# Output projection of a hybrid decoder layer: the recurrence half computed ahead of and among the first attention steps

## The reference, cut to what matters

```
h = rmsnorm(x, norm_g) * (1 + scale) + shift        # shift, scale, gate from c
z = h @ w_in                                        # xr, gr, q, k, v, ga, qi, ki, wi
y_r = rg_lru(conv(xr)) * silu(gr)                   # 512 channels, a recurrence along the sequence
y_a = dsa_attention(q, k, v, qi, ki, wi) * silu(ga) # 8 heads of 64, top-256 keys by an index score
y = concat([y_r, y_a], axis=-1) @ w_out             # 1024 x 1024
x = x + gate * y
return rmsnorm(x, final_g)
```

## Time and profile before

| what | value |
|---|---|
| time, median of 3 runs | 620.57 us (620.45 to 621.84) |
| profiled execution | 619.93 us, span 618.1 us |
| mean granted TensorE clock | 0.926 |
| busy: PE / DVE / ACT / POOL | 535.4 / 439.5 / 377.4 / 233.5 us |
| first transposes of stage 2 | 365.76 us |
| scores of step 16 (first of tile 4) | 406.32 us |
| scores of step 24 (first of tile 7) | 437.19 us |
| last matmul of the output projection ends | about 610.8 us |

### The profile page before, as it was taken

One profiled execution on the slowest core, in us unless ns is written; L12 is line 12 of the kernel. 1 busy time (PEld: TensorE's weight loads), 2 busy tenths in 40 slices (PEclk: granted clock), 3 DMA queues, 4 the chain that ended last, 5 costly groups with the idle time before them and its releaser, 6 DMA issues.

```text
span 618.1 us, 8029 instructions
## 1 busy us (share of the span) xinstructions
PE 535.4 (87%) x2676; PEld 444.8 (72%) x2676; DVE 439.5 (71%) x992; ACT 377.4 (61%) x679; POOL 233.5 (38%) x195
## 2 busy tenths in 40 slices
PE   1459989998999999999999526489999999999994
PEld 1346868777787777778888415478889999888873
DVE  5987386885999889898697886854475666664522
ACT  6513236453499999987898555554466666656531
POOL 5150862352344274677642003740402030313322
PEclk9859999998999999999999855569999999999999
DMA  8967342430112111135550420110011000101011
GB/s 335 418 206 266 105 118 53 102 85 18 36 34 69 34 36 34 35 103 137 140 133 0 177 96 0 68 36 2 8 61 43 28 36 34 41 30 69 0 69 68
DMA packets 16457, 51.96 MB, mean 84 GB/s; under 512 B 4000, under 2 KB 5024, under 8 KB 15392
## 3 DMA queue, kind: packets, MB, share of 16 engines
q1 hardware_dynamic: 16416, 51.45, 26.3%
HBM read 37.81 MB, written 4.19 MB: 68 GB/s over the span
## 4 chain that ended last, share of the span: by engine, by line
PE 68%; DVE 11%; DMA 7%; POOL 5%; ACT 4%; issue 3%; SPq 2%; DVEq 0%; POOLq 0%; ACTq 0%
PE pair L1373 30%; PE pair L1470 13%; PE pair L1492 6%; PE pair L1505 5%; DMA ada<-in_ada_w 4%; PE pair L1448 3%; PE pair L1449 2%; DMA qs<-half_lo 2%; PE pair L1422 2%; DVE rank L1156 2%; PE pair L1514 2%; PE pair L1413 2%; PE pair L1414 2%; DVE tie L1158 1%; POOL half_lo L726 1%
## 5 line engine op out<-in xcount | busy, mean ns | idle before, releaser
L1373 PE MATMUL pair<-h_hi,w_hi 128*128 128x512 f32 (+1 forms) x352 | 114.4, 407 | 1.6 <-DVE h_lo L1064 1.5
L1373 PE MATMUL pair<-h_lo,w_hi 128*128 128x512 f32 (+1 forms) x352 | 109.8, 393 | 0.0
L1373 PE MATMUL pair<-h_hi,w_lo 128*128 128x512 f32 (+1 forms) x352 | 109.0, 391 | 0.0
L1298 DVE TENSOR_TENSOR pt_lo<-pair,pt_hi 128x512 fp32r<-128x512 f32 (+3 forms) x96 | 50.5, 554 | 71.1 <-ACT pt_hi L963 70.5
L858 ACT ACTIVATE bias_sb<-score_sb,tinies 128x1024 bf16<-128x1024 f32 (+2 forms) x93 | 95.7, 1032 | 3.2 <-DVE tinies L1109 3.1
L696 POOL TENSOR_SCALAR w_hi<-w_raw 128x1024 fp32r<-128x1024 f32 (+1 forms) x22 | 29.4, 1339 | 136.3 <-PE pair L1373 120.5
L1373 PEld LDWEIGHTS pair<-h_hi,w_hi 128*128 128x128 f32 (+1 forms) x352 | 65.0, 188 | 19.0 <-issue 6.2
L1373 PEld LDWEIGHTS pair<-h_lo,w_hi 128*128 128x128 f32 (+1 forms) x352 | 66.0, 188 | 15.5 <-issue 0.8
L1373 PEld LDWEIGHTS pair<-h_hi,w_lo 128*128 128x128 f32 (+1 forms) x352 | 65.6, 186 | 15.4 <-issue 0.7
L1095 DVE TENSOR_SCALAR_CACHE_REDUCE bias_sb<-score_sb,tinies 128x640 bf16<-128x640 f32 (+2 forms) x93 | 72.6, 802 | 0.9
L781 POOL TENSOR_TENSOR x_res<-q_free,x_res 128x512 f32<-128x512 f32 x14 | 18.1, 1296 | 121.0 <-DVE q_free L1269 121.0
(11 more groups left out here) (195 smaller groups left out, 1254.2 us busy)
## 6 DMA issues: line engine op xcount, KB each, us to landing
w_raw<-in_w_tiles SPq DMA_DIRECT2D x21, 512.0 KB, 3.5
ada<-in_ada_w SPq DMA_DIRECT2D x8, 1024.0 KB, 18.4
x_sb<-in_x SPq DMA_DIRECT2D x8, 512.0 KB, 7.1
ada_g<-in_ada_w SPq DMA_DIRECT2D x8, 512.0 KB, 4.5
qs<-half_hi SPq DMA_DIRECT2D x16, 256.0 KB, 3.6
qs<-half_lo SPq DMA_DIRECT2D x16, 256.0 KB, 4.4
wo_raw<-in_w_out SPq DMA_DIRECT2D x8, 512.0 KB, 6.4
x_res<-in_x SPq DMA_DIRECT2D x8, 512.0 KB, 3.3
```

Source lines behind the costliest of these rows:

```text
L1298: nc.vector.tensor_tensor(pt_lo[:, 4 * b:4 * b + nc4, hh, :], psum[use % 2][:, 0:nc4 * P].rearrange("p (c q) -> p c q", q=P), f32(pt_hi[:, ...
L1373: ins = nc.tensor.matmul(psum[banks[half]][0:width, :], w[b][:, k, 0:width], hh[:, k, half * HALF:(half + 1) * HALF], start=(k == 0 and p ...
```

## The change

The recurrence half (m < 4) leaves the pieces. For each tile ti and column half it becomes a part of 12 matmuls, e = 2 ti + half, 16 parts. Parts 0 to 3 stand on TensorE ahead of step 0, part g+4 in step g for g = 0 to 11, behind the scores. ScalarE copies each part to SBUF, SP stores it in the rows of the output, where the final result will later overwrite it. In stage 2 the stored rows are loaded back, GpSimd multiplies them with the gate and adds them to x_res (base_of), and what follows is as before. The pieces now hold m = 4 to 7: four a tile, one in every second step from 8 ti + 14 on, for the last tile one a step in 70 to 73. w_out's hi for the slabs 0 to 3 is made by GpSimd, for 4 to 7 by ScalarE in steps 2 to 5. yr_hi of the first two tiles is made at the end of stage 1. The diff, cut to its core:

```diff
-WO_START = 5
-OUT_START = 20
-PIECES = {g: [2 * (g - OUT_START), 2 * (g - OUT_START) + 1] for g in range(OUT_START, 2 * OUT_START - LAG_OUT)}
-PIECES.update({g: [g - LAG_OUT] for g in range(2 * OUT_START - LAG_OUT, LAST_STEP)})
+FIRST_PARTS = 4
+PARTS = 2 * NT
+WO_POOL = CT
+WO_START = 2
+PIECES = {8 * ti + LAG_OUT + 1 + (2 * p if ti < NT - 1 else p): [4 * ti + p] for ti in range(NT) for p in range(4)}
...
+        add("ACT", ("yrh", b), 0.7, 1, ("kstep", NJ - 2 + b, KC - 1), ("yr", CT - 1))
...
+        def part_bank(e):
+            return 2 if e < FIRST_PARTS and e % 2 else 3
...
@@ sync @@
+            for e in range(PARTS):
+                ti, half = divmod(e, 2)
+                i = ATT[ti]
+                sp.wait_ge(part_ev, e + 1)
+                sp.dma_start(out[i * P:(i + 1) * P, half * HALF:(half + 1) * HALF], part[half][:, :]).then_inc(part_out[half], 16)
+            def part_load(ti):
+                i = ATT[ti]
+                for half in range(2):
+                    sp.wait_ge(part_out[half], 16 * (ti + 1))
+                sp.dma_start(part_in[ti % 2][:, :], out[i * P:(i + 1) * P, :]).then_inc(part_back[ti % 2], 16)
...
+            sp.wait_ge(part_ps, PARTS)
             for ti in range(2):
                 sp.dma_start(x_res[ti][:, :], x[ATT[ti] * P:(ATT[ti] + 1) * P, :]).then_inc(xres_in[ti], 16)
+                part_load(ti)
...
                     sp.dma_start(x_res[ti % 2][:, :], x[nxt * P:(nxt + 1) * P, :]).then_inc(xres_in[ti % 2], 16)
+                    sp.wait_ge(base_ok, ti + 1)
+                    part_load(ti + 2)
@@ gpsimd @@
+            def split_wo(m):
+                if m < WO_POOL:
+                    pool.wait_ge(wo_in[m], 16)
+                    nc.gpsimd.tensor_scalar(wo_hi[:, m, :], wo_raw[:, m, :], 1.0, 0.0, ALU.mult, ALU.add).then_inc(wo_hi_ok, 1)
+                pool.wait_ge(wo_hi_ok, m + 1)
+                nc.gpsimd.tensor_tensor(wo_lo[:, m, :], wo_raw[:, m, :], f32(wo_hi[:, m, :]), ALU.subtract).then_inc(wo_ok, 1)
             split_yr(0)
-            split_yr(1)
+            for m in range(WO_POOL):
+                split_wo(m)
+            for ti in range(1, 4):
+                split_yr(ti)
+            for ti in range(4, NT):
+                split_wo(ti)
+                split_yr(ti)
+            def base_of(ti):
+                b = ti % 2
+                pool.wait_ge(part_back[b], 16 * (ti // 2 + 1))
+                nc.gpsimd.tensor_tensor(part_in[b][:, :], part_in[b][:, :], gate_bc[:, :], ALU.mult).then_inc(part_mul, 1)
+                pool.wait_ge(xres_in[b], 16 * (ti // 2 + 1))
+                pool.wait_ge(part_mul, ti + 1)
+                nc.gpsimd.tensor_tensor(x_res[b][:, :], x_res[b][:, :], part_in[b][:, :], ALU.add).then_inc(base_ok, 1)
+            base_of(0)
...
                     nc.gpsimd.tensor_tensor(xs, xs, fg_bc, ALU.mult).then_inc(fin_ok, 1)
+                    base_of(ti + 1)
@@ scalar @@
+            def part_evac(e):
+                ti, half = divmod(e, 2)
+                act.wait_ge(part_ps, e + 1)
+                if ti:
+                    act.wait_ge(part_out[half], 16 * ti)
+                nc.scalar.activation(part[half][:, :], bank(part_bank(e)), ACT.Copy).then_inc(part_ev, 1)
+                if half and ti + 2 < NT:
+                    yr_half(ti + 2)
+            for e in range(FIRST_PARTS - 1):
+                part_evac(e)
             for g in range(LAST_STEP + 1):
+                if 0 <= g + FIRST_PARTS - 1 < PARTS:
+                    part_evac(g + FIRST_PARTS - 1)
...
@@ vector @@
                         if half == 0:
-                            dve.wait_ge(xres_in[ti % 2], 16 * (ti // 2 + 1))
+                            dve.wait_ge(base_ok, NT)
@@ tensor @@
+            def part_of(e):
+                ti, half = divmod(e, 2)
+                i = ATT[ti]
+                if e < 2:
+                    pe.wait_ge(evac_done, len(EVAC) - 1)
+                elif e <= FIRST_PARTS:
+                    pe.wait_ge(part_ev, e - 1)
+                else:
+                    pe.wait_ge(part_ev, e)
+                if half == 0:
+                    pe.wait_ge(yr_ok, ti + 1)
+                for m in range(CT):
+                    if e == 0:
+                        pe.wait_ge(wo_ok, m + 1)
+                    y2 = (yr_hi[ti % 2][:, m, :], yr_lo[:, m, i * P:(i + 1) * P])
+                    for p, (y, w) in enumerate(((y2[0], wo_hi), (y2[0], wo_lo), (y2[1], wo_hi))):
+                        ins = nc.tensor.matmul(bank(part_bank(e)), y, w[:, m, half * HALF:(half + 1) * HALF],
+                                               start=(m == 0 and p == 0), stop=(m == CT - 1 and p == 2))
+                ins.then_inc(part_ps, 1)
+            for e in range(FIRST_PARTS):
+                part_of(e)
...
                     ins.then_inc(att_ps, 1)
+                if g + FIRST_PARTS < PARTS:
+                    part_of(g + FIRST_PARTS)
```

More of the change, by code:

```diff
@@ L227, in stages @@
     add("DVE", ("prep",), 3.5, 2, ("nonneg", len(PICK) - 1))
+    for b in range(2):
+        add("ACT", ("yrh", b), 0.7, 1, ("kstep", NJ - 2 + b, KC - 1), ("yr", CT - 1))
     add("ACT", ("sign",), 3.0, 2, (("prep",), -2.5))
@@ L402, in layer_kernel @@
         x_res = [sb("x_res0", R_R, [P, D]), sb("x_res1", R_S, [P, D])]
-        yr_hi = [sb(f"yr_hi{b}", R_S + 4096 + 2048 * b, [P, CT, P], F32R) for b in range(2)]
+        yr_hi = [sb(f"yr_hi{b}", R_W + 18432 + 2048 * b, [P, CT, P], F32R) for b in range(2)]
+        part = [sb(f"part{b}", R_W + 12288 + 2048 * b, [P, HALF]) for b in range(2)]
         pv_sb = [sb(f"pv{b}", R_R + 4096 + 1024 * b, [P, 2, P]) for b in range(2)]
@@ L419, in layer_kernel @@
         yr_lo = sb("yr_lo", R_YR, [P, CT, S], F32R)
+        part_in = [sb(f"part_in{b}", R_YR + 4096 * b, [P, D]) for b in range(2)]
         ga = sb("ga", R_GA, [P, 4, S])
@@ L548, in layer_kernel @@
         yr_ok = sem("yr_ok")
+        part_ps = sem("part_ps")
+        part_ev = sem("part_ev")
+        part_out = [sem(f"part_out{b}") for b in range(2)]
+        part_back = [sem(f"part_back{b}") for b in range(2)]
+        part_mul = sem("part_mul")
+        base_ok = sem("base_ok")
         att_ps = sem("att_ps")
@@ L663, in _ @@
                     sp.dma_start(x_res[ti % 2][:, :], x[nxt * P:(nxt + 1) * P, :]).then_inc(xres_in[ti % 2], 16)
+                    sp.wait_ge(base_ok, ti + 1)
+                    part_load(ti + 2)
             sp.wait_ge(out_dma, 16 * (NT + 1))
+            for half in range(2):
+                sp.wait_ge(part_out[half], 16 * NT)
         @block.gpsimd
@@ L776, in _ @@
                 if ti < NT - 1:
[L777 removed]
+                    pool.wait_ge(base_ok, ti + 1)
                     for half in range(2):
@@ L958, in _ @@
                         act.wait_ge(pv_ps, pair)
+                    if g - LAG_T == 16:
+                        for b in range(2):
+                            act.wait_ge(part_out[b], 16 * NT)
                     for b in range((keys_of(i) + HALF - 1) // HALF):
@@ L973, in _ @@
                 for o in PIECES.get(g - 1, ()):
-                    if o % 8 == 7 and o // 8 < NT - 1:
-                        ti = o // 8
+                    if o % 4 == 3 and o // 4 < NT - 1:
+                        ti = o // 4
                         act.wait_ge(rstd1_ok, ti + 1)
@@ L979, in _ @@
                 for o in PIECES.get(g, ()):
-                    if o % 4 != 3:
+                    if o % 2 == 0:
                         continue
-                    ti, half = divmod(o // 4, 2)
+                    ti, half = divmod(o // 2, 2)
                     if ti < NT - 1:
@@ L1296, in _ @@
                         nc4 = min(4, i + 1 - 4 * b)
+                        if g - LAG_T == 16 and b == 0:
+                            dve.wait_ge(part_ps, PARTS)
                         dve.wait_ge(t_hi, use_t(use) + 1)
@@ L1450, in _ @@
                     ins.then_inc(att_ps, 1)
+                if g + FIRST_PARTS < PARTS:
+                    part_of(g + FIRST_PARTS)
                 for o in PIECES.get(g, ()):
-                    ti, piece = divmod(o, 8)
-                    i = ATT[ti]
-                    half = piece // 4
-                    if piece % 4 == 0:
-                        if 2 * ti + half:
+                    ti, piece = divmod(o, 4)
+                    half = piece // 2
+                    if piece % 2 == 0:
+                        if o == 0:
+                            pe.wait_ge(part_ev, PARTS)
+                            pe.wait_ge(wo_ok, KC)
+                        else:
                             pe.wait_ge(y_ok, 2 * ti + half)
-                    if ti == 0 and piece < 4:
-                        pe.wait_ge(wo_ok, 2 * piece + 2)
                     if piece == 0:
-                        pe.wait_ge(yr_ok, ti + 1)
-                    if piece == 2:
                         pe.wait_ge(ya_ok, ti + 1)
-                    for m in (2 * (piece % 4), 2 * (piece % 4) + 1):
```

(12 more changed lines are left out.)

35 lines of the change are left out of this document (14 added, 21 removed).

## The result

The changed kernel takes 649.01 us (median of 4 runs, 647.45 to 650.24) where the kernel before takes 620.51 us beside it (619.54 to 621.84): ratio 1.0456, 95% interval 1.0427 to 1.0486, so 28.5 us slower. The forecast was 644.6 us, with a range of 626 to 668. The profiled execution took 649.02 us, with a span of 647.2 us.

What follows compares the result with a forecast made beforehand. The prediction took TensorE to bound the kernel, except in a half-clock hole in attention steps 0 to 15. 620.57 us + 41 (later step 16) - 17 (given back) = 644.6 us, range 626 to 668.

Steps and rivals of the forecast that it cites:

- Step 1: From attention step 16 on: 43.8 us of matmuls leave, odd steps wait for o_sb, 17 us gained (8 to 46).
- Rival (b): Full stretch: odd steps close up because o_sb comes earlier, all 46 us arrive, 616 us; chance 0.07.
- The stand: Tile 7's odd steps: without the piece, TensorE waits 0.87 us for o_sb before the values product.
- Step 2: Start, four parts ahead of step 0: fourth slab ready at 368, transposes of step 1 at 386.4 instead of 365.8.
- the contention price: Start: a w_out slab costs GpSimd 4.6 us beside VectorE's masks, taken three times, against 3.4 alone.
- Step 3: Early attention steps: one part per step without overlap, so step 16 starts 41 us later (33 to 52).
- the ring: Early steps: part, transposes, pt_hi, exponent, evacuation in series, 4.8 us a round; 53.0 us from part 5 to part 15.
- rival (c): Early steps fall to the 1.2 GHz level: 27 us more, 671 us; chance 0.13.
- the way out: From the end of part 15 (439.4) to the start of step 16 (447.4): 8.0 us at full clock.
- Step 4: Loading back, late tiles and end: GpSimd's base_of delays the last add, so 5.5 us fewer matmuls give only 0.5.
- (a): Early steps: the hole hides the parts, only the start's 21 us is lost, 625 us; chance 0.07.
- (d): Whole kernel: parts aren't earlier, or the order differs from what was read: 620 within 2; chance 0.02.

Runs made afterwards that it cites:

- e2: Changed kernel with the recurrence half of the output projection left out altogether, including its stores, loads back and w_out splits: 596.85 us.
- e4: Changed kernel with GpSimd making base_of of the next tile between a tile's two residual adds instead of behind fin: 643.65 us.
- e1: Changed kernel with ScalarE evacuating part g+4 in step g, ahead of pt_hi, instead of in step g+1 behind the exponent: 633.95 us.
- e5: Changed kernel with the four wo_hi copies moved from the end of steps 2 to 5 to directly behind the evacuation: 640.67 us.
- e7: Changed kernel with the first four parts made into four banks at once, row block by row block, and the second tile's recurrence output split first: 641.96 us.
- e10: Changed kernel with four more matmuls, results unused, in each of steps 0 to 14, ahead of the part: 646.05 us.

## Why the prediction held, step by step

**Step 1** (17 us given back) held in mechanism and nearly in size: 14.5 us measured. Tile 4 gained 4.4 (4.4 forecast), tile 7 6.0 (5.9), tiles 6 and 5 2.6 (3.4), tile 3 1.0 (1.0). The term that was most off is the last, tile 2 with the end: 0.5 against 1.9. Rival (b), all 46 us, fell in e2: 24 us even with nothing added. The stand that the forecast read from the rows of tile 7 (0.87 us) came as 0.78: 481.50 less the 480.72 at which the scores' last matmul gave up its place. The idle time that it announced for the values product, some 25 us, came as 16.7, with 5.0 more ahead of the Y transposes.

**Step 2** (start) was pessimistic. The first three blocks cost GpSimd 3.4 us each and the fourth 4.6: ready at 366.1, not 368. The term that failed is the contention price, applied three times, where only the last block paid it. The masks began at 359.20, beside the third block's subtraction, and there it was VectorE that was slow (the same instruction on 512 keys took 0.28 us):

```profile
359.17 2.35 POOL L806 TENSOR_TENSOR wo_lo<-wo_raw,wo_hi 128x1024 fp32r<-128x1024 f32 x1
359.20 2.50 DVE L1222 TENSOR_SCALAR tie<-bias_sb 128x640 bf16<-128x640 bf16 x1
...
362.69 3.39 POOL L806 TENSOR_TENSOR wo_lo<-wo_raw,wo_hi 128x1024 fp32r<-128x1024 f32 x1
```

Part 0 ended at 367.6 (369.5 forecast), and the transposes of step 1 came at 384.2 (386.4). What the Trainium skill says (GPSIMD Engine Reference, section 1) on sharing with VectorE was seen on the last block, 3.39 us instead of 2.35, and on VectorE's side in e4 (2.31 instead of 0.69 us). The forecast's upper price for all four blocks, 378 us, was not met. It rested in part on a row that doesn't bear on it: the 3.10 us of the earlier trace rows for a copy like line 696 was taken at 218.6 us, beside VectorE's bisection and recurrence, not beside a mask.

**Step 3** (the ring) held: ten rounds, part 5 at 381.30 to part 15 at 436.61, took 55.3 us where 53.0 were forecast, and e1 shows that the ring is what makes them long. The missing term is the clock, which was assumed at 1.00 and fell to 0.50 in two of the rounds, at 1.6 us a part (4.61 against 3.02), and again in steps 12 to 15: part 15's end to step 16 took 10.3 instead of 8.0 us. Where the clock held, in e4, e5 and e7, the same way took 8.1 us. (It also holds the first piece of the output projection, in step 14, which the forecast doesn't name.) That is a piece of rival (c), whose price, 27 us, was that of a fall in all the rounds. The row of 412 to 416 in the earlier trace rows with its full clock was taken as the general case, and the gap was reckoned at 1 us for every round. In the four steps with a wo_hi copy it was 1.7 to 2.2 us. Of these four parts two came at half clock:

```profile
391.61 0.79 PE L1520 MATMUL pair<-wo_hi,yr_hi 128*128 128x512 f32 x1 [2.15 <-ACT part L1000]
399.37 0.50 PE L1520 MATMUL pair<-wo_hi,yr_hi 128*128 128x512 f32 x1 [2.21 <-ACT part L1000]
405.00 0.56 PE L1520 MATMUL pair<-wo_hi,yr_hi 128*128 128x512 f32 x1 [1.71 <-ACT part L1000]
412.76 0.50 PE L1520 MATMUL pair<-wo_hi,yr_hi 128*128 128x512 f32 x1 [2.21 <-ACT part L1000]
```

The first and the third are the slow ones (0.79 and 0.56 for the first matmul, 4.61 for the part). The Trainium skill (TensorE: Matmul & The Clock Gate, "HAM oscillation") describes this falling back between bursts; the trace agrees for these two rounds and not for the other eight. Together the early terms made step 16 start 43.6 us later, 41 forecast: part 5 came 2.4 us earlier than forecast, the ring took 2.3 more, the way out 2.3 more, and part 15 itself 0.3 more. That this sum came so near is in part luck: the start was too dear by about what the fall of the clock in the way out cost.

**Step 4** (loading back) held in its place and order. In the trace fin, base_of and the add follow each other without a gap, as reckoned, and the one delayed square that reaches TensorE costs it 1.2 us (at 622.3 us, 1 forecast). Against e2 it costs 7.9 us, in the last tile and the end. From the end of that fin to the end of the span both kernels take 12.7 us, so the end gave nothing; the forecast booked 0.5 us for it, although its own two figures, 611.8 and 611.57, say 0.2 us lost. Tile 2 up to there gained 0.5 us where 1.4 were forecast; what took the other 0.9 us is open. The case that x_res comes late, which made the lower bound of step 1, did occur once the early steps were shorter: in tile 4 of e4, e5 and e7.

**Rivals (a) and (d)** fall by the timeline: from part 5 on the parts start 4.4 to 7.8 us apart, not 3.

## What to carry to other kernels

Filling an engine's idle time with another stage's work costs what the queues around it make of it: write down, for each engine in its program order, what the moved work waits for and what waits behind it, and look for a ring that returns to itself once per step. Then ask of every instruction taken out of a full stretch which wait it was covering; half of a line with 97 us of busy time was worth 24 us here, with nothing put in its place. And make the pieces small enough to begin on what has arrived: the same four parts, one row block at a time, ended 8 us earlier, and 5.5 us of that were left at the last part. Last, before a gain is put down to an edit, see whether a stretch that the edit doesn't touch has changed too: 2.3 us came and went with the clock in steps 12 to 15.

## What the runs showed of the hardware

- The granted clock fell from 2.4 to 1.2 GHz after some gaps of TensorE (2.15 and 1.71 us) and held through others as long (2.21 us, twice); no run here tells what makes the difference. It isn't the length of the gap alone: in e4, whose early steps are the same, it fell at the two gaps of 2.22 us (parts of 4.4 us) and held through those of 2.15 and 1.71. In e5 (gaps ahead of a part up to 1.3 us) and e10 it held in all of steps 0 to 15, and e10 did 60 matmuls more in less time.
- VectorE's smallest operations suffer beside GpSimd too. An operation on three elements a partition took 2.14 us beside a wo_lo split, and ended with it, where another of the same shape took 0.16:

```profile
355.95 2.14 DVE L1210 SCALAR_TENSOR_TENSOR tinies<-tinies 128x3 f32<-128x3 f32 x1
...
359.12 0.16 DVE L1214 SCALAR_TENSOR_TENSOR tinies<-tinies 128x3 f32<-128x3 f32 x1
```
